# Ten row buffers and VectorE's diagonals in a two-block kernel whose expert gather runs beside everything else

## The reference, cut to what matters

```
s1, s2 = q @ keys1, q @ keys2              # 8 heads, 128 keys each
idx, gates = top 16 of the sums of the two top 16
u  = take(expert_down, idx)                # 128 rows of 1024 for each token
act = gelu(einsum('bpd,bphkd->bphk', h, u))
vv = take(expert_up, idx)                  # 128 more rows for each token
out = einsum('bphk,bphkd->bpd', gates * act, vv)
```

## Time and profile before

| | |
|---|---|
| median of 3 runs | 4658.88 us (4643.64 to 4669.87) |
| the profiled execution's own time | 4644.1 us |
| its span, first to last instruction | 4642.3 us |
| mean granted TensorE clock | 0.796 of full speed |
| busy: TensorE, VectorE, ScalarE, GpSimd | 68%, 55%, 19%, 25% of the span |
| DMA of the gather's queue | 1073.81 MB, 58.6% of 16 engines' span |

### The profile page before, as it was taken

One profiled execution on the slowest core, in us unless ns is written; L12 is line 12 of the kernel. 1 busy time (PEld: TensorE's weight loads), 2 busy tenths in 40 slices (PEclk: granted clock), 3 DMA queues, 4 the chain that ended last, 5 costly groups with the idle time before them and its releaser, 6 DMA issues. The chain is left out here.

```text
span 4642.3 us, 46965 instructions
## 1 busy us (share of the span) xinstructions
PE 3168.6 (68%) x16550; PEld 1624.6 (35%) x16550; DVE 2544.3 (55%) x6284; ACT 876.3 (19%) x2385; POOL 1158.9 (25%) x1028
## 2 busy tenths in 40 slices
PE   4966587874565565786588674686768885556666
PEld 3843486562121111442255441342335551111111
DVE  5547766347644677445544357544643437755554
ACT  1113100221111111114411111112522011111111
POOL 0000000001433344223222233232312224344443
PEclk8988798986677777887699886786889987766666
DMA  4510000224988899887688787786778888899998
GB/s 169 185 49 3 4 1 8 73 73 169 394 338 341 352 412 414 322 315 290 251 330 337 275 317 317 275 330 220 260 258 337 331 317 339 353 387 420 419 420 361
DMA packets 202518, 1249.21 MB, mean 269 GB/s; under 512 B 24940, under 2 KB 29420, under 8 KB 67572
## 3 DMA queue, kind: packets, MB, share of 16 engines
q0 software_dynamic: 147456, 1073.81, 58.6%
q1 hardware_dynamic: 54328, 172.55, 10.4%
q10 hardware_dynamic: 512, 0.03, 0.0%
HBM read 1241.79 MB, written 4.46 MB: 268 GB/s over the span
## 5 line engine op out<-in xcount | busy, mean ns | idle before, releaser
L221 POOL DMA_INDIRECT held_pair<-in_experts,held_expert x1024 | 1158.7, 1132 | 3454.0 <-PE held_acc L241 2253.3
L241 PE MATMUL held_acc<-held_pair,held_diag 64*64 64x512 f32 x8192 | 1413.7, 789 | 622.3 <-ACT held_diag L267 559.5
L287 DVE CUSTOM_DVE_ANT_0 held_pair<-held_pair,held_hrow 128x1024 f32<-128x1024 f32 x1024 | 1247.6, 1222 | 739.5 <-DMA held_pair<-in_experts,held_expert 653.5
L241 PEld LDWEIGHTS held_acc<-held_pair,held_diag 64*64 64x64 f32 x8192 | 276.2, 159 | 1524.8 <-ACT held_diag L267 1267.1
L267 ACT ACTIVATE held_diag<-held_bands,held_weight 128x64 f32<-128x64 f32 x1024 | 347.8, 340 | 1598.6 <-DVE held_weight L282 1576.6
L260 ACT ACTIVATE held_bent<-held_dot 128x2 f32<-128x2 f32 x512 | 103.9, 203 | 746.7 <-DVE held_dot L287 659.3
L598 PE MATMUL pgh_ps<-held_hT,pgh_w 128*128 128x256 f32 x768 | 181.8, 391 | 28.0 <-DMA pgh_w<-in_w_in 28.0
L598 PE MATMUL p2h_ps<-held_hT,p2h_w 128*128 128x256 f32 x736 | 175.9, 393 | 31.3 <-DMA p2h_w<-in_w_in 31.3
L598 PEld LDWEIGHTS pgh_ps<-held_hT,pgh_w 128*128 128x128 f32 x768 | 144.6, 193 | 82.2 <-issue 34.1
L598 PEld LDWEIGHTS p2h_ps<-held_hT,p2h_w 128*128 128x128 f32 x736 | 139.4, 194 | 86.8 <-issue 35.7
L598 PE MATMUL e2qh_ps<-held_hT,e2qh_w 128*128 128x256 f32 x512 | 124.1, 397 | 23.4 <-DMA e2qh_w<-in_w_peer_q 23.4
(11 more groups left out here) (482 smaller groups left out, 3865.4 us busy)
## 6 DMA issues: line engine op xcount, KB each, us to landing
pgh_w<-in_w_in SPq DMA_DIRECT2D x48, 512.0 KB, 7.3
p2h_w<-in_w_in SPq DMA_DIRECT2D x46, 512.0 KB, 7.5
p_raw<-in_w_in SPq DMA_DIRECT2D x34, 512.0 KB, 3.6
p_w_ada<-in_w_ada SPq DMA_DIRECT2D x16, 1024.0 KB, 6.5
held_pair<-in_experts,held_expert POOLq DMA_INDIRECT x1024, 9.8
e2qh_w<-in_w_peer_q SPq DMA_DIRECT2D x32, 512.0 KB, 7.1
ada_w<-in_w_ada SPq DMA_DIRECT2D x4, 2048.0 KB, 10.6
e1q_raw<-in_w_query SPq DMA_DIRECT2D x16, 512.0 KB, 3.5
```

What stands on the lines that cost most here:

```text
L221: pool.indirect_dma_start(self.pair[m % BUFS][:], None, self.layers[t // TT][0], bass.IndirectOffsetOnAxis(ap=self.expert[:, t % TT, s:s + ...
L241: last = pe.matmul(self.sum_of(i)[to * BAND:(to + 1) * BAND], diag[band, :], up[band, turn * WIDE:(turn + 1) * WIDE], start=s == 0, stop=s ...
L287: ins = dve.tensor_tensor_reduce(down, down, self.hrow[:, t % TT, :], 1.0, 0.0, ALU.mult, ALU.add, self.dot[:, t % 2, s:s + 1])
```

## The change

The buffers `pair` grow from 8 to 10 and the diagonals go from 6 to 5. VectorE writes each diagonal itself, at beat n that of slot n-3, from `bent` and `gate` as its two scalars; the product `weight` and ScalarE's copy are gone. VectorE waits for the gelu at the first slot of a pair, and for the up of slot n-8 before it writes over a diagonal. TensorE does the up of slot n-3 at beat n (`UP_AT` = 3), and GpSimd the gather of slot n+7 (`AHEAD` = 7), for which it waits for the up of slot n-3.

To find room for the buffers, some tiles of the second mixer's stages (the five row tiles of each attention, `pick` of the head norms, the forget gate's five vectors, `fq`) are put into parts of `room` and `hT` that are not in use then. The instructions on them stay the same.

```
-GROUP, BUFS, DIAGS = 2, 8, 6
+GROUP, BUFS, DIAGS = 2, 10, 5
 BENT_AT = GROUP
-WEIGH_AT = GROUP + 1
-DIAG_AT = WEIGH_AT
-UP_AT = DIAG_AT + 1
+DIAG_AT = GROUP + 1
+UP_AT = DIAG_AT
 AHEAD = BUFS - UP_AT
...
     def act(self, act, n):
...
-        m = n - DIAG_AT
-        if 0 <= m < SLOTS:
-            t, s = divmod(m, NJ)
-            act.wait_ge(self.weighed, m // GROUP + 1)
-            if m >= DIAGS:
-                act.wait_ge(self.added, m - DIAGS + 1)
-            act.activation(self.diag[m % DIAGS][:], self.k.bands[:], ACT.Copy, scale=self.weight[:, t % 2, s:s + 1]).then_inc(self.diag_made, 1)
...
     def dve(self, dve, n):
-        g, s = divmod(n - WEIGH_AT, GROUP)
-        if s == 0 and 0 <= g < SLOTS // GROUP:
-            t, q = divmod(g, NJ // GROUP)
-            at = slice(q * GROUP, (q + 1) * GROUP)
-            dve.wait_ge(self.bent_made, g + 1)
-            dve.tensor_tensor(self.weight[:, t % 2, at], self.bent[:, t % 2, at], self.gate[:, t % TT, at], ALU.mult).then_inc(self.weighed, 1)
+        m = n - DIAG_AT
+        if 0 <= m < SLOTS:
+            t, s = divmod(m, NJ)
+            if s % GROUP == 0:
+                dve.wait_ge(self.bent_made, m // GROUP + 1)
+            if m >= DIAGS:
+                dve.wait_ge(self.added, m - DIAGS + 1)
+            dve.tensor_scalar(self.diag[m % DIAGS][:], self.k.bands[:], self.bent[:, t % 2, s:s + 1], self.gate[:, t % TT, s:s + 1],
+                              ALU.mult, ALU.mult).then_inc(self.diag_made, 1)
...
-            attention_stage(nc, own("mema"), k, items, GH, GD, memT, loads=[(mkv[:], memory)], beats=beats["mema"])
+            attention_stage(nc, own("mema"), k, items, GH, GD, memT, loads=[(mkv[:], memory)], beats=beats["mema"],
+                            spare=[room[:, c, :] for c in [Y_GATE] + list(range(3 * DC + 4, 4 * DC))])
...
-MIXER_LENGTHS = {"n3": 5, "p2": 35, "hn": 15, "vt": 2, "forget": 9, "foxa": 28, "swaa": 18, "mema": 8, "pg": 36, "mg": 20, "po": 13, "n4": 5,
-                 "q": 24, "choose": 40}
+MIXER_LENGTHS = {"n3": 7, "p2": 28, "hn": 20, "vt": 4, "forget": 11, "foxa": 33, "swaa": 24, "mema": 12, "pg": 29, "mg": 19, "po": 12, "n4": 7,
+                 "q": 20, "choose": 40}
```

More of the change, by code:

```diff
@@ L755, in _, with attention_stage @@
                 dve.tensor_copy(kk[:, :, :, NOPE:QH], bcast(kr[:], MH, 2)).then_inc(heads, 1)
-def attention_stage(nc, name, k, items, heads, vdim, oT, sinks=None, loads=(), saves=(), beats=None):
+def attention_stage(nc, name, k, items, heads, vdim, oT, sinks=None, loads=(), saves=(), beats=None, spare=()):
     per = P // vdim
@@ L770, in attention_stage @@
         r = Room(nc, stack, name)
-        p = [r.sb(f"p{u}", [P, 512]) for u in range(3)]
-        pT = [r.sb(f"pT{u}", [P, 512]) for u in range(2)]
+        tiles = list(spare) + [r.sb(f"p{u}", [P, 512])[:] for u in range(5 - len(spare))]
+        p, pT = tiles[0:3], tiles[3:5]
         nmax, total, inv = r.sb("nmax", [P, N]), r.sb("total", [P, N]), r.sb("inv", [P, N])
@@ L1494, in _, with head_norm_stage @@
             beats.dve(dve, 0)
-def head_norm_stage(nc, name, row_pick, chunks, tokens=S, beats=None):
+def head_norm_stage(nc, name, row_pick, chunks, tokens=S, beats=None, spare=None):
     N = len(chunks)
@@ L1521, in _ @@
             def _(sp):
-                sp.dma_start(pick[:], row_pick[0:2 * N, 0:N, :]).then_inc(loaded, 16)
+                sp.dma_start(pick, row_pick[0:2 * N, 0:N, :]).then_inc(loaded, 16)
             @block.scalar
@@ L1612, in _, with forget_stage @@
                     beats.dve(dve, n)
-def forget_stage(nc, name, k, z, bias, fq, fk, low, last_sum, cols, beats):
+def forget_stage(nc, name, k, z, bias, fq, fk, low, last_sum, cols, beats, spare):
     beats = beats.over(2)
@@ L1620, in forget_stage @@
         r = Room(nc, stack, name)
-        v, least, mag, c, ones = [r.sb(n, [FH, tokens]) for n in ("v", "least", "mag", "c", "ones")]
+        v, least, mag, c, ones = [spare[:, u, :] for u in range(5)]
         raised, absed, logged, summed, filled, moved, chain = r.sem("raised", "absed", "logged", "summed", "filled", "moved", "chain")
@@ L1718, in second_mixer @@
     z, gates = room[:, 0:Y_GATE, :], room[:, 0:3 * DC, :]
+    spare = [room[:, Y_GATE + 2 * u:Y_GATE + 2 * u + 2, :].rearrange("p a n -> p (a n)") for u in range(4)]
     foxT, swaT, memT = hT[:, 0:4, other], hT[:, 4:8, other], room[:, 3 * DC:3 * DC + 4, :]
@@ L1728, in second_mixer @@
         heads += [(z[:, Y_MQ + i, :], cols("mem_q_g"), GD, GD ** -0.5, z[:, Y_MQ + i, :]) for i in range(4)]
-        head_norm_stage(nc, own("hn"), ins["row_pick"], heads, tokens=HALF, beats=beats["hn"])
+        head_norm_stage(nc, own("hn"), ins["row_pick"], heads, tokens=HALF, beats=beats["hn"],
+                        spare=room[:, Y_GATE:, :].rearrange("p a n -> p (a n)"))
         tiles = range(first, first + HTILES)
@@ L1734, in second_mixer @@
             a = Room(nc, fox, own("fox"))
-            fq, fk = a.sb("fq", [66, FH // 2, HALF]), a.sb("fk", [66, FH // 2, now.stop])
+            fq, fk = swaT[0:66], a.sb("fk", [66, FH // 2, now.stop])
             lanes = lambda head: slice(head % 2 * 64, head % 2 * 64 + 2)
-            forget_stage(nc, own("forget"), k, z, cols("b_forget")[0:FH], fq[:], fk[:], past.low, past.last_sum, now, beats["forget"])
+            forget_stage(nc, own("forget"), k, z, cols("b_forget")[0:FH], fq, fk[:], past.low, past.last_sum, now, beats["forget"], room[0:FH, Y_GATE:, :])
             items = []
@@ L1745, in second_mixer @@
             kept = [(fox_k[:, :, 0:HALF], past.fox_k), (swa_k[:, 0:HALF], past.swa_k), (v[:, :, 0:HTILES, :], past.v)]
-            attention_stage(nc, own("foxa"), k, items, FH, FD, foxT, beats=beats["foxa"],
+            attention_stage(nc, own("foxa"), k, items, FH, FD, foxT, beats=beats["foxa"], spare=spare,
                             loads=kept if half else [], saves=[] if half else [(there, here_) for here_, there in kept])
@@ L1758, in second_mixer @@
                                   alibi[:, head, (0 if t else P):2 * P], [v[:, 4, j, part] for j in range(k0, t + 1)], head, t - first, None))
-            attention_stage(nc, own("swaa"), k, items, SH, SD, swaT, sinks=sinks, beats=beats["swaa"],
+            attention_stage(nc, own("swaa"), k, items, SH, SD, swaT, sinks=sinks, beats=beats["swaa"], spare=spare,
                             loads=[(alibi[:], ins["alibi"]), (sinks[:], ins["swa_sinks"].to_broadcast([P, SH]))])
```

9 lines of the change are left out of this document (5 added, 4 removed).

## The result

The changed kernel takes 4880.72 us (median of 4 runs, 4879.15 to 4884.77) against 4655.92 us of the kernel before (4 runs, 4643.64 to 4669.87). The ratio is 1.0489, with a 95% interval of 1.0468 to 1.0510. It is slower by 225 us. Its profiled execution took 4879.15 us with a span of 4877.3 us, 235 us more than that of before.

The account below looks back on a forecast made before the run. DMA bounds the choosing stage and drain, TensorE and DMA nearly fill projections, other stages' own chains and landing-bound barriers set the rest. Terms -54 + 91 + 113 + 5 = +155 us gave 4800 us, range 4665 to 4890.

Parts of the forecast that it names:

- likeliest case: Whole kernel: the forecast itself, 4735 to 4860 us, by the diagonal's time and the clock in hn and swaa; chance 0.55.
- rival (c): Attentions and mg: turn-taking lowers TensorE's activity and its clock, 85 us on top, 4885 us; chance 0.10.
- Single signs: Profile after: n3 near 27 us, p2 8 shorter, swaa some 20 longer, mg some 12 longer, drain within 10 of 546.8.
- Two more buffers, +5 us: Look-ahead 7 for 4: one stock of three slots built in the first hosted stage, less one gather, +5 us.
- Beats that leave and arrive, +37 us: Moved beats: -54 us from projections and a choosing stage, +91 us in norms, head norms, attentions and other stages.
- The diagonal on VectorE: One VectorE instruction per slot, taken as 0.25 us, hidden under the 2.5 us gather in DMA-bound stages.
- The slack, +113 us: foxa, swaa, mema, mg, hn, vt: without a beat between diagonal and use, TensorE and VectorE take turns; bounds nothing and 200 us.
- (a): Stage boundaries: the look-ahead hides the barrier's wait, 82 us, and the slack term is nil; about 4600 us; chance 0.13.
- (b): TensorE's beats: the diagonals are ready in time, leaving only -54 + 91 + 5, 4686 us; chance 0.13.
- (d): DMA-bound stretches: VectorE's new instruction slows GpSimd's descriptor writing, 114 us more, 4913 us; chance 0.03.
- (e): Whole kernel: gains and losses cancel within half a per cent; chance 0.06.

Follow-up runs that it names:

- experiment 11: The kernel before with VectorE's diagonals in place of ScalarE's, eight buffers, slack and old beats kept, and AHEAD = 2: 4489.32 us, ratio 0.9648.
- experiment 2: The changed kernel with the old lengths of the beats; ten buffers, VectorE's diagonals and the missing slack stay: 4842.57 us, ratio 1.0393.
- experiment 1: The changed kernel with UP_AT one beat later than DIAG_AT again, look-ahead 6 for 7, new beats kept: 4675.35 us, ratio 1.0042.
- experiment 5: The changed kernel with the beat of slack back and the old beats, ten buffers, look-ahead 6: 4642.51 us, ratio 0.9991.
- experiment 3: The kernel before with UP_AT = DIAG_AT alone, look-ahead held at 4, eight buffers, ScalarE's diagonals, old beats: 4819.09 us, ratio 1.0344.

## Why the prediction was right, and where it was off

The sign, the stages and most of the mechanism came out; the time is 81 us above the forecast, outside the likeliest case's own range (4735 to 4860) and inside the wide one, near the 4885 of rival (c). It lies inside because the range took rival (c) in: the sum by itself had 155 of the 225 us. Single signs: n3 28.6 us for "near 27", p2 7.4 us shorter for 8, mg 12.3 longer for 12, the drain 3.6 longer; but swaa 32.5 us longer for "some 20".

- **Two more buffers, +5 us.** Right as far as it was measured, from look-ahead 4 to 6: +7 us, not told from nothing; the step from 6 to 7 was only run together with the slack. The two reasons held: the barrier follows the last landing (10.8 us at swaa's end), and the first gather of a stage waits for TensorE. What the prediction did not see is that the same buffers pay 173 us once they are not all spent on look-ahead. The Trainium skill's sentence on a repeated gap (Perfetto Trace Analysis, Optimization Strategy) was set aside for the drain, where too few buffers are not the cause: 550.4 us with ten and 546.8 with eight. Nor are they for the gap at every boundary: as depth two more gave nothing, and with eight buffers and look-ahead 2 most of the gap goes (experiment 11).
- **Beats that leave and arrive, +37 us.** About right: 38 to 45 us by experiment 2, 24 (ratios) to 33 (medians) between experiments 1 and 5. p2 lost 7.4 us for 8, n3 gained 6.9 for 5, hn 11.1 for about 13 with its slack term.
- **The diagonal on VectorE.** Taken as 0.25 us and 0.311 in the trace, and hidden in the DMA-bound stages, as said. The prediction gave it no gain; alone it gained 0.25%.
- **The slack, +113 us: the mis-sized term.** It measured 208 us (experiment 1), 187 with the old beats; the upper bound that was given for it, 200 us, was too low with the new ones. In mg 0.85 us a beat was predicted; TensorE waited 14.7 us for the diagonal in 17 beats, 0.86, and the stage grew 12.3 us for the 12 foreseen. The step of foxa at the higher clock was predicted at 5.46 us and took 5.57, but that step is one of 16: their mean is 6.87 us, and 4.97 with the slack back. foxa and swaa were sized at 53 us in the two halves; between experiment 1 and the changed kernel they are 113. The step that failed is the assumption there that TensorE's clock stays where it was. 66 of the 113 us are busy time that the same matmuls took more, and the 47 that are left stand against the 53 of the prediction. So rival (c), put at 0.10, came true in part: in foxa and swaa, not in mg. Against experiment 1 over both halves, mg (29 foreseen, 31 measured), mema (11, and 9) and hn with vt (20, and 17) were about right. Some 32 us lie in stages for which the prediction had nothing of this term: forget, the norms, the choosing stages and the first layer.
- **Rivals.** (a) The boundaries did not shrink with look-ahead 7; the quiet at the 28 stage starts is 290 us, for 249 before; fallen. (b) The diagonals are not in time: TensorE waits 16.3 us for them in foxa of the second half alone; fallen. (d) The gather's issue slowed by 0.06 us in the drain (1.11 us for 1.05), far from the 2.5 us of a gather, and the drain grew 3.6 us; fallen as a cost. (e) Nothing cancelled but the 0.25%.

That the clock fell because of the turn-taking is shown as far as putting one beat back, with the same matmuls, restored it (0.54 to 0.82, 0.69 to 0.78), and as far as taking it out of the kernel before lowered it too (0.73 to 0.53 in swaa of the second half). TensorE's activity was not varied by itself.

## What to carry to other kernels

A producer and a consumer that wait on each other in the same step of two in-order streams need a step between them, even when both have idle time: here one beat is worth 187 to 208 us, and buffers spent on depth don't make up for it. Where a stage ends in a barrier, count a look-ahead queue twice, once for depth and once for how early the first and last transfers of the stage may be issued; buffers held free over the boundary gave 3.7%, the same buffers as depth gave nothing, and eight buffers with less depth and two held free gave 3.3%. When a change makes TensorE wait in every step, price its matmuls at the lower clock as well: in foxa and swaa 47 us of loss became 113.

## What the runs showed of the hardware that was not expected

- The clock can cost as much as the waits that go with its fall. One swaa stage of 304 matmul records took 55.83 us of TensorE's time at a granted clock of 0.82 and 83.78 us at 0.54. TensorE's waits for the diagonal came to 3.2 us before 3 of the 22 ups in the first case and 17.6 us before 16 of them in the second.
- mg, with 0.86 us of wait before each of its 17 beats, kept its clock (0.93 against 0.91). Its TensorE was busy 65.99 of 90.74 us, 0.73; that of swaa in the second half with the slack back 55.83 of 84.68 us, 0.66, also kept it (0.82), while the same swaa in the changed kernel, 83.78 of 118.37 us, 0.71, lost it (0.54). So the busy share of a whole stage does not tell which level it will get. The Trainium skill (TensorE: Matmul & The Clock Gate, Part 1) has the clock halved unless the engine has been busy lately, in two levels only; the up at 1.09 and 1.98 us agrees with the two levels.
- Without slack ScalarE's diagonal came later than VectorE's although ScalarE was busy 18% of the span of that kernel (experiment 3): the place of the work in an engine's stream counted, not the engine's load (2.75 us of waiting in a step against 0.77).
- With VectorE's 1024 diagonals a gather's issue on GpSimd took 1.11 to 1.13 us in the drain, with ScalarE's 1.05 to 1.06.
